# Attention stage on half slots: the two maps of a unit apart, negated maxima, roots on VectorE, the second half's units further apart

## The chip, the cores and the metric

One Trainium2 chip, one of its cores. The metric is the device time of one execution in microseconds; lower is better. TensorE (PE), VectorE (DVE), ScalarE (ACT), GpSimd (POOL) and the DMA queues run at the same time; each works through its own instruction list in order and waits for the others through semaphores. SyncE (SP) only issues transfers here.

## The reference, cut to what matters

One layer on 512 prompt positions and on 8 samples of 16 positions each (with 256 cached positions), D_MODEL 1024, float32:

```python
h = rms_norm(x, norm1_g) * (1 + sc1) + sh1
proj = h @ w_in                        # 11264 columns: retention q k v gate, diff q k v, two gates
ret_o = rms_norm(retention(...)) * silu(rg)
dq = rope(rms_norm(dq, diff_qnorm_g)); dk = rope(rms_norm(dk, diff_knorm_g))   # groups of 64
# differential attention: 8 heads, two maps per head (64 columns each), values 128 wide
s = einsum(q, k) * 64 ** -0.5          # per map; masked block-causally, chunks of 64
p = softmax(s); a = p[map 0] - lam * p[map 1]; diff_o = a @ v
diff_o = rms_norm(diff_o, diff_subln_g) * (1 - lam_init)
merged = sigmoid(g0) * (ret_o @ w_br_ret) + sigmoid(g1) * (diff_o @ w_br_diff)
x = x + gt1 * (merged @ w_out)
h2 = rms_norm(x, norm2_g) * (1 + sc2) + sh2
x = x + gt2 * hierarchical_moe(h2, ...)   # 16 experts, top-1 group, top-2 experts
```

The rotated keys, the values and the retention states are outputs as well.

## The kernel before, in words

The program has a retention phase (`phase_r`), then `phase_d`, which holds the attention stage, the output projection with the second norm and the router, and the experts. The change lies in the attention stage of `phase_d`, from about 777 us to 1190 us of the span.

**Groups, steps and slots.** In that stage TensorE works through nine projection groups (`DIFF_GROUPS`: K0, V0, Q1, K1, V1, GD0, GD1, BR0, BR1), each 512 columns wide: the diff-attention keys, values and queries of head halves 0 and 1 (four heads each; Q0 comes from the phase before), the gate of that branch in two halves, and the branch's output projection in two halves. A group has 8 row blocks k times 5 row tiles t (4 of the prompt, 1 of all samples) = 40 steps. A step (`step`, `mm3`) is three matmuls of 128x128 by 128x512 in split single precision (high x high, high x low, low x high) into bank `pj[t]`. Weights arrive in pieces of 128 x 1024 values, of which ScalarE makes the high part (`split_hi`) and GpSimd the low part by a subtraction (L1889).

Two steps are a slot; 20 slots are a group. Ahead of every slot TensorE calls `attend(s)`, and the other engines walk through the same slots, so the attention work is laid between the projection steps by a timetable written out by hand: class `Attention`, one object for each head half. For a slot it tells which unit is scored, turned, valued and so on. The class `Jobs` walks through the same slots once and numbers all the small TensorE jobs, each with one of the three small banks `B[0..2]` and its turn in it; `job_done` waits until TensorE has finished a job, `job_taken` until its bank was read. Since every engine's list is in slot order, an instruction that waits holds all that stands behind it on its engine.

**A unit** is one head and one query tile: 16 for each half, unit u has head u % 4, query tile u // 4 and (u // 4 + 1) x 128 keys.
- `scores` (L2430 on): for both maps a matmul with 64 rows of contraction (partitions 0 to 63 for map 0, 64 to 127 for map 1) and a mask matmul over the last 64 keys, into banks 0 and 1; the two maps' matmuls stand next to each other in the list.
- `maxima` (VectorE): two reduces and one scaling by -SCALE (L2172, L2174). `exps` (ScalarE): two exponentials with row sums (L1946), map 1 always into `E[:, 2]`, map 0 into `E[:, u % 2]`. `combine` (VectorE, L2180 to L2182): reciprocals, lambda factor, and the weighted sum of both maps.
- `turn` (TensorE, L2448): transposes; `take_A` (ScalarE, L1954) copies them; `values` (L2458) multiplies by the values; `take_o` (VectorE, L2190) scales into `o`; `square_o` (ScalarE, L1961) sums squares for the norm.

Half 0 scores a unit every 2 slots from slot 42 on, half 1 every slot from slot 102 on; the turn comes 3 and 2 slots after the scores, the values one slot later.

**The samples** follow unit 15 of each half, eight of them every two slots: `turn_keys` transposes 256 cached keys, `s_scores`, `s_maxima`, `s_exp`, `s_scale`, `s_turn`, `s_fold`, and for each pair of samples `s_values`. Cached keys and values come by transfers (`load_kc`, `load_vc`) into one buffer each.

**Rows and norms.** Q and K groups are taken out of the banks by ScalarE (`take_rows`, a square and a copy for each tile), summed by VectorE (`head_squares`), rooted (ScalarE's Sqrt, then `rsqrt_steps` on VectorE, L115 to L123) and rotated (`rotate`, one tile every two slots), then transposed at the slots in `turns`. The output norm does the same for each half in two parts (`o_variance`, `o_root`, `o_norm_root`, `o_norm`), and `out` has the slots at which its tiles are transposed for the branch projection. ScalarE loads a function table (ACT_TABLE_LOAD) whenever it goes from Exp, Sigmoid or Sqrt to another of these.

## Time and profile before

| | us |
|---|---|
| median of 3 runs | 1673.2 (1672.86 to 1677.64) |
| profiled execution | 1674.01 |
| its span | 1672.2 |
| TensorE busy | 1519.2 (91%) |
| VectorE busy | 825.7 (49%) |
| ScalarE busy | 665.5 (40%) |
| GpSimd busy | 355.2 (21%) |

The span runs from the first to the last instruction; the device time has 1.8 us more around it. The durations of matmuls are modelled and overlap in the pipeline (a 512-wide projection matmul shows 0.39 us), so cost is read from the start of one to the start of the next. The mean granted TensorE clock of the span is 0.960 of full speed. In the profile PE is the matmuls, PEld the weight loads; `d_B` are the small banks, `d_sm` the unit's maxima and sums, `d_E` the maps, `d_AT` the turned map, `ring_*` the weight pieces.

### The profile page before, as it was taken

What the parts mean: (1) busy time and instruction counts of PE and PEld (TensorE: products, weight loads), DVE (VectorE), ACT (ScalarE), POOL (GpSimd) and SP (SyncE); (2) the same over time, 40 slices, a digit from 0 to 9 for tenths busy, and PEclk for the clock granted to TensorE, in tenths of its full rate; (3) what the DMA queues carried; (4) which work ended last, traced back from release to release, by engine and by line L of the source; (5) the groups of instructions that cost most, each with busy time, mean ns of one, the idle gap of its engine ahead of it and who ended that gap; (6) DMA issues with size and microseconds to landing.
All of it is one profiled execution on the core that took longest, in us unless ns stands there. A gap on an engine that the chain in (4) does not pass through costs nothing.

```text
span 1672.2 us, 21251 instructions
## 1 busy us (share of the span) xinstructions
PE 1519.2 (91%) x7820; PEld 1140.6 (68%) x7820; DVE 825.7 (49%) x1370; ACT 665.5 (40%) x1085; POOL 355.2 (21%) x197
## 2 busy tenths in 40 slices
PE   4999999999999999997998788889999699999991
PEld 3675777577747764786875566767778578877871
DVE  3332341234123312222846664643445689998894
ACT  5312311221123112322344343564222268888881
POOL 1341123123312321333331111111430300000002
PEclk8999999999999999998999999999999599999995
DMA  9434452346136423424331144124661499999985
GB/s 342 127 89 139 149 181 73 126 152 197 53 126 194 157 78 131 158 76 151 94 114 38 39 139 145 58 77 152 251 172 51 132 337 360 392 394 390 386 326 201
DMA packets 158091, 290.31 MB, mean 174 GB/s; under 512 B 15084, under 2 KB 40860, under 8 KB 157734
## 3 DMA queue, kind: packets, MB, share of 16 engines
q1 hardware_dynamic: 154246, 278.47, 49.3%
q0 software_dynamic: 3744, 10.49, 1.7%
q8 instruction: 64, 1.05, 0.3%
q14 instruction: 37, 0.30, 0.1%
HBM read 251.55 MB, written 40.52 MB: 175 GB/s over the span
## 4 chain that ended last, share of the span: by engine, by line
PE 28%; DMA 9%; DVE 8%; ACT 4%; issue 3%; SPq 1%; DVEq 0%; ACTq 0%; POOL 0%; POOLq 0%
PE pj L93 7%; PE pj L95 7%; PE pj L94 7%; DMA m_raw<-w 6%; DVE d_tmp L2161 1%; DVE d_sm L2172 1%; ACT d_E L1946 1%; PE d_B L2439 1%; PE d_B L2466 1%; PE d_B L2500 1%; ACT m_hi L1362 1%; DMA d_kc<-cache_diff_k 1%; PE d_B L2458 1%; PE d_B L1537 1%; PE d_B L2477 1%
## 5 line engine op out<-in xcount | busy, mean ns | idle before, releaser
L93 PE MATMUL pj<-ring_hi,hT_hi 128*128 128x512 f32 x880 | 370.5, 421 | 20.6 <-ACT d_q_rows L1924 9.9
L95 PE MATMUL pj<-ring_hi,hT_lo 128*128 128x512 f32 x880 | 348.8, 396 | 0.0
L94 PE MATMUL pj<-ring_lo,hT_hi 128*128 128x512 f32 x880 | 348.2, 396 | 0.0
L464 POOL TENSOR_TENSOR ring_lo<-ring_raw,ring_hi 128x1024 fp32r<-128x1024 f32 x79 | 190.9, 2418 | 555.1 <-ACT ring_hi L530 555.1
L530 ACT ACTIVATE ring_hi<-ring_raw 128x1024 fp32r<-128x1024 f32 x79 | 83.5, 1059 | 427.8 <-DMA ring_raw<-w_in 361.9
L1441 DVE TENSOR_TENSOR m_lo<-m_raw,m_hi 128x1024 fp32r<-128x1024 f32 x188 | 224.2, 1222 | 23.9 <-ACT m_hi L1362 21.3
L93 PEld LDWEIGHTS pj<-ring_hi,hT_hi 128*128 128x128 f32 x880 | 168.5, 191 | 80.3 <-issue 34.7
L1362 ACT ACTIVATE m_hi<-m_raw 128x1024 fp32r<-128x1024 f32 x188 | 194.2, 1058 | 26.6 <-DMA m_raw<-w 24.1
L95 PEld LDWEIGHTS pj<-ring_hi,hT_lo 128*128 128x128 f32 x880 | 167.9, 191 | 37.9
L94 PEld LDWEIGHTS pj<-ring_lo,hT_hi 128*128 128x128 f32 x880 | 169.0, 192 | 30.4 <-issue 1.0
L1889 POOL TENSOR_TENSOR ring_lo<-ring_raw,ring_hi 128x1024 fp32r<-128x1024 f32 x37 | 89.9, 2433 | 362.8 <-ACT ring_hi L1909 362.8
L719 DVE SCALAR_TENSOR_TENSOR r_S<-r_S,g,r_sm 128x512 f32<-128x512 f32 x64 | 45.3, 745 | 124.1 <-PE r_sm L969 124.0
L93 PE MATMUL pj<-m_hi,m_xT_hi 128*128 128x512 f32 x248 | 98.8, 398 | 0.0
L95 PE MATMUL pj<-m_hi,m_xT_lo 128*128 128x512 f32 x248 | 97.2, 392 | 0.0
L94 PE MATMUL pj<-m_lo,m_xT_hi 128*128 128x512 f32 x248 | 97.1, 391 | 0.0
L93 PE MATMUL pj<-ring_hi,r_oT_hi 128*128 128x512 f32 x160 | 64.5, 403 | 5.0 <-issue 5.0
L1909 ACT ACTIVATE ring_hi<-ring_raw 128x1024 fp32r<-128x1024 f32 x37 | 39.1, 1057 | 73.1 <-DMA ring_raw<-w_in 25.5
L1335 POOL DMA_INDIRECT m_xe<-xg,m_si x16 | 16.5, 1033 | 240.7 <-PE d_B L1529 222.3
L94 PE MATMUL pj<-ring_lo,r_oT_hi 128*128 128x512 f32 x160 | 62.6, 391 | 0.0
L95 PE MATMUL pj<-ring_hi,r_oT_lo 128*128 128x512 f32 x160 | 62.4, 390 | 0.0
L1946 ACT ACTIVATE d_E<-d_B,d_sm 128x128 f32<-128x128 f32 (+3 forms) x64 | 33.2, 524 | 62.0 <-DVE d_sm L2174 62.0
L95 PEld LDWEIGHTS pj<-m_hi,m_xT_lo 128*128 128x128 f32 x248 | 46.9, 189 | 10.1
(341 smaller groups left out, 2428.4 us busy)
## 6 DMA issues: line engine op xcount, KB each, us to landing
m_raw<-w SPq DMA_DIRECT2D x188, 512.0 KB, 10.8
ring_raw<-w_in SPq DMA_DIRECT2D x72, 512.0 KB, 3.8
r_S<-state_ret SPq DMA_DIRECT2D x64, 256.0 KB, 4.7
r_ada_raw<-w_ada SPq DMA_DIRECT2D x16, 1024.0 KB, 6.7
o_state_s<-r_S SPq DMA_DIRECT2D x64, 256.0 KB, 4.8
a_raw<-w_ada SPq DMA_DIRECT2D x8, 1024.0 KB, 11.9
ring_raw<-w_in SPq DMA_DIRECT2D x32, 256.0 KB, 3.1
ring_raw<-w_br_ret SPq DMA_DIRECT2D x16, 512.0 KB, 4.0
```

Source lines behind the costliest of these rows:

```text
L93: pe.matmul(out, s_hi, m_hi, start=start, stop=False)
L94: pe.matmul(out, s_hi, m_lo, start=False, stop=False)
L95: return pe.matmul(out, s_lo, m_hi, start=False, stop=stop)
L464: pool.tensor_tensor(lo[:, p], raw[:, p], hi[:, p].bitcast(F32), ALU.subtract).then_inc(lo_done, 1)
L530: act.activation(hi[:, p], raw[:, p], ACT.Copy).then_inc(hi_done, 1)
L719: dve.scalar_tensor_tensor(S[:, u % 8], S[:, u % 8], K.g16[:, h:h + 1], job_bank("U", h, u)[:], ALU.mult, ALU.add) \
L1362: act.activation(self.hi[self.slot(n)][:], self.raw[self.slot(n)][:], ACT.Copy).then_inc(self.hi_done, 1)
L1441: dve.tensor_tensor(self.lo[s][:], self.raw[s][:], self.hi[s][:].bitcast(F32), ALU.subtract).then_inc(self.lo_done, 1)
L1537: last = pe.transpose(self.AT[:, a * P:(a + 1) * P], self.su[:, a * P:(a + 1) * P], K.ident[:])
L1889: pool.tensor_tensor(lo[:, p], raw[:, p], hi[:, p].bitcast(F32), ALU.subtract).then_inc(lo_done, 1)
L1909: act.activation(hi[:, p], raw[:, p], ACT.Copy).then_inc(hi_done, 1)
L1946: act.activation(E[:, u % 2 if m == 0 else 2, 0:nk], job_bank("S", i, u, m)[:, 0:nk], ACT.Exp, scale=SCALE, bias=sm[:, u % 4, 2 + m:3 + m] ...
```

## The change

The timetable counts in steps (half slots, 0 to 359) instead of slots. `place(h)` gives the old slot for even h and -2 for odd h, so work tied to a slot of a group stays where it was. In half slots, counted from the first scores of a unit:

| | before, half 0 | before, half 1 | after, both |
|---|---|---|---|
| map 1 / map 0 scored | 0 / 0 | 0 / 0 | 0 / 1 |
| combined | 2 | 2 | 3 |
| turned | 6 | 4 | 6 |
| valued | 8 | 6 | 8 |
| first unit, distance | 84, 4 | 204, 2 | 84, 4 and 194, 3 |

The samples' stream of half 1 starts at 246 (was 240); from the turn of a sample's keys, scores come at 3 (2), turn at 9 (6), values at 17 (14). The last output tile of half 1 is turned at 302 (298). `SCALE` goes into the query gains, so neither the exponentials nor the maxima scale; the maximum reduces write negated values themselves. Map 1's exponentials go to `E[:, 2]` and, for odd units, into half of the cached-value buffer `vc`, which is therefore loaded only after the last unit is combined. Every inverse root of the stage is made on VectorE from a bit pattern and three Newton steps, without ScalarE's Sqrt. Gate half 0 (GD0) is copied raw at the start of GD1, and both gate halves get their sigmoid at the start of BR0. GpSimd's `block_q` for half 1 moves from group GD1 to GD0.

```diff
+def rsqrt_bits(dve, links, out, var, tmp):
+    links(dve.tensor_scalar(tmp.bitcast(I32), var.bitcast(I32), 1, None, ALU.logical_shift_right))
+    links.sync()
+    links(dve.tensor_scalar(out.bitcast(I32), tmp.bitcast(I32), -1.0, float(0x5F3759DF), ALU.mult, ALU.add))
+    links.sync()
+    for _ in range(3):
+        links(dve.scalar_tensor_tensor(tmp, out, -0.5, out, ALU.mult, ALU.mult))
+        links.sync()
+        links(dve.tensor_tensor(tmp, tmp, var, ALU.mult))
+        links.sync()
+        links(dve.scalar_tensor_tensor(out, tmp, 1.5, out, ALU.add, ALU.mult))
+        links.sync()
...
-SLOTS = 20
+STEPS = KT * NT
+BETWEEN = -2
+def place(h):
+    return DIFF_GROUPS[h // STEPS], h % STEPS // 2 if h % 2 == 0 else BETWEEN
...
-        self.first, self.step, self.lag = ((42, 2, 3), (102, 1, 2))[i]
-        self.cache = (76, 120)[i]
+        self.first, self.period = ((84, 4), (194, 3))[i]
+        self.cache = (152, 246)[i]
...
+    def scored(self, h, m):
+        return self.unit(h, 1 - m)
+    def combined(self, h):
+        return self.unit(h, 3)
+    def turned(self, h):
+        return self.unit(h, 6)
+    def valued(self, h):
+        return self.unit(h, 8)
...
+        def exp_of(u, m):
+            return E[:, u % 2] if m == 0 else E[:, 2] if u % 2 == 0 else vc[:, 1, 0]
...
                     j = half.s_valued(s)
-                    if some(j) and (j + 1 < DEC_B // 2 or i == 0):
-                        load_vc(*((i, j + 1) if j + 1 < DEC_B // 2 else (1, 0)))
+                    if some(j) and j + 1 < DEC_B // 2:
+                        load_vc(i, j + 1)
+                    if half.combined(s) == U - 1:
+                        sp.wait_ge(A_done, (i + 1) * U)
+                        load_vc(i, 0)
...
-                    elif name in ("GD1", "BR0"):
-                        j = int(name == "BR0")
-                        take(f"GD{j}", lambda t: sg[:, t, j * W:(j + 1) * W], ACT.Sigmoid)
+                    elif name == "GD1":
+                        take("GD0", lambda t: sg[:, t, 0:W], ACT.Copy)
+                    elif name == "BR0":
+                        take("GD1", lambda t: sg[:, t, W:], ACT.Sigmoid)
+                        for t in range(NT):
+                            bank_taken(act, "GD0", t)
+                            act.activation(sg[:, t, 0:W], sg[:, t, 0:W], ACT.Sigmoid).then_inc(gate_done, 1)
...
                     if some(half.turned(s)):
                         take_A(i, half.turned(s))
-                    if some(half.scored(s)):
-                        exps(i, half.scored(s))
+                    for a in (1, 0):
+                        if some(half.scored(s, a)):
+                            exps(i, half.scored(s, a), a)
+                    if some(half.valued(s - 3)):
+                        n = half.valued(s - 3)
+                        square_o(i, n, o[i][:, n // HH, n % HH * P:(n % HH + 1) * P])
...
-            def maxima(i, u):
-                nk, c = unit_of(u)[2], sm[:, u % 4]
-                for m in range(2):
-                    job_done(dve, "S", i, u, m)
-                    links(dve.tensor_reduce(c[:, m:m + 1], job_bank("S", i, u, m)[:, 0:nk], AX, ALU.max))
-                links.sync()
-                dve.tensor_scalar(c[:, 2:4], c[:, 0:2], -SCALE, None, ALU.mult).then_inc(nmax_done, 1)
+            def maximum(i, u, m):
+                job_done(dve, "S", i, u, m)
+                dve.tensor_reduce(sm[:, u % 4, 2 + m:3 + m], job_bank("S", i, u, m)[:, 0:unit_of(u)[2]], AX, ALU.max, negate=True) \
+                   .then_inc(nmax_done, 1)
...
-            def scores(i, u):
+            def scores(i, u, m):
...
-                for m in range(2):
-                    pe.matmul(out[m][:, 0:nk], qT[i][part[m], h, t * P:(t + 1) * P], kT[i][part[m], h, 0:nk], start=True, stop=False)
-                for m in range(2):
-                    pe.matmul(out[m][:, nk - CHUNK:nk], mp[part[m], 0:P], mp[part[m], P:P + CHUNK], start=False, stop=True).then_inc(done, 1)
+                out, part = small("S", i, u, m), slice(m * DDH, (m + 1) * DDH)
+                pe.matmul(out[:, 0:nk], qT[i][part, h, t * P:(t + 1) * P], kT[i][part, h, 0:nk], start=True, stop=False)
+                pe.matmul(out[:, nk - CHUNK:nk], mp[part, 0:P], mp[part, P:P + CHUNK], start=False, stop=True).then_inc(done, 1)
...
             def attend(s):
                 for half in halves:
                     i = half.i
+                    for m in (1, 0):
+                        if some(half.scored(s, m)):
+                            scores(i, half.scored(s, m), m)
                     if some(half.valued(s)):
                         values(i, half.valued(s))
...
-                        if (k * NT + t) % 2 == 0:
-                            attend(g * SLOTS + (k * NT + t) // 2)
+                        attend(g * STEPS + k * NT + t)
```

## Rows read from the trace of the kernel before

**Rows 1.** Table by stretch, us: busy time and count per engine, clock, DMA share, GB/s.
```profile
849.64:890.13 40.49, 37.69 (x214) 29.16 (x212) 17.58 (x58) 17.13 (x60) 9.47 (x4) 1.00 0.26 83
890.13:952.89 62.76, 46.91 (x234) 33.54 (x233) 43.92 (x89) 26.78 (x73) 7.80 (x3) 0.92 0.09 26
952.89:1036.82 83.93, 72.22 (x614) 54.23 (x612) 49.23 (x121) 34.59 (x74) 12.18 (x5) 0.92 0.42 132
1036.82:1113.33 76.51, 65.45 (x411) 52.00 (x410) 40.29 (x115) 44.43 (x134) 10.88 (x6) 0.99 0.24 77
1113.33:1168.82 55.49, 53.98 (x528) 40.94 (x526) 24.05 (x76) 25.72 (x52) 9.53 (x4) 0.98 0.46 143
1168.82:1189.42 20.60, 18.88 (x94) 15.39 (x92) 5.42 (x15) 7.87 (x13) 4.81 (x2) 1.00 0.48 176
```
**Rows 2.** Timeline of TensorE at 793 us: start us, duration us, engine, line, operation.
```profile
793.16 0.39 PE L93 MATMUL pj<-ring_hi,hT_hi 128*128 128x512 f32 x1
...
793.85 0.39 PE L93 MATMUL pj<-ring_hi,hT_hi 128*128 128x512 f32 x1
```
**Rows 3.** Timeline of weight loads around the scores of two units (256, 512 keys).
```profile
871.68 0.30 PEld L2439 LDWEIGHTS d_B<-d_kT,d_qT 64*128 64x128 f32 x4
...
872.48 0.19 PEld L93 LDWEIGHTS pj<-ring_hi,hT_hi 128*128 128x128 f32 x1
...
932.94 0.97 PEld L2458 LDWEIGHTS d_B<-d_v,d_AT 128*128 128x128 f32 x8 [1.78 <-ACT d_AT L1954]
...
934.03 0.30 PEld L2439 LDWEIGHTS d_B<-d_kT,d_qT 64*128 64x128 f32 x4
...
935.26 0.19 PEld L93 LDWEIGHTS pj<-ring_hi,hT_hi 128*128 128x128 f32 x1
```
**Rows 4.** Timeline of weight loads of one sample slot.
```profile
1011.21 0.38 PEld L2500 LDWEIGHTS d_B<-d_vc,d_ATs 128*32 128x32 f32 x16 [0.36 <-issue]
...
1012.66 0.31 PEld L2487 LDWEIGHTS d_B<-ident,d_Ps 128*128 128x128 f32 x3 [0.20 <-issue]
1013.14 0.16 PEld L2477 LDWEIGHTS d_B<-d_kcT,d_qB 128*32 128x32 f32 x8 [0.17 <-issue]
...
1014.34 0.19 PEld L93 LDWEIGHTS pj<-ring_hi,hT_hi 128*128 128x128 f32 x1
```
**Rows 5.** Waits of 777 to 1210 us: waiter, releaser: total us, times, longest.
```profile
ACT d_E L1946 <- DVE d_sm L2174: 62.0, 29, 6.3
ACT d_Ps L1977 <- DVE d_sms L2198: 48.7, 16, 4.8
...
PE d_B L2458 <- ACT d_AT L1954: 14.7, 9, 4.9
```
**Rows 6.** Timeline of VectorE between the starts of two rotations, 512 keys.
```profile
933.28 1.29 DVE L2161 TENSOR_TENSOR d_tmp<-d_q_rows,d_tabs 128x512 f32<-128x512 f32 x2
...
936.27 1.28 DVE L2172 TENSOR_REDUCE d_sm<-d_B 128x1 f32<-128x512 f32 x2
...
939.33 0.17 DVE L2180 RECIPROCAL d_sm<-d_sm 128x2 f32<-128x2 f32 x1 [1.58 <-ACT d_E L1946]
...
940.46 1.29 DVE L2161 TENSOR_TENSOR d_tmp<-d_q_rows,d_tabs 128x512 f32<-128x512 f32 x2
```
**Rows 7.** Timeline, all engines, around one of GpSimd's subtracts.
```profile
872.27 2.40 POOL L1889 TENSOR_TENSOR ring_lo<-ring_raw,ring_hi 128x1024 fp32r<-128x1024 f32 x1 [7.13 <-ACT ring_hi L1909]
...
872.58 0.76 DVE L2172 TENSOR_REDUCE d_sm<-d_B 128x1 f32<-128x256 f32 x2 [0.44 <-PE d_B L2441]
...
873.37 1.32 DVE L2174 TENSOR_SCALAR d_sm<-d_sm 128x2 f32<-128x2 f32 x1
```
**Rows 8.** Groups of ScalarE, 777 to 1210 us: busy us, mean ns, idle before.
```profile
L1983 ACT ACT_TABLE_LOAD x4 | 5.1, 1283 | 0.1
```
**Rows 9.** Timeline of ScalarE, gate tiles of GD1.
```profile
1165.48 1.78 ACT L1931 ACTIVATE d_sg<-pj 128x512 f32<-128x512 f32 x3
```
**Rows 10.** Chain of waits, the transfer of a sample's cached keys.
```profile
989.39 4.92 DMA d_kc<-cache_diff_k
```

More of the change, by code:

```diff
@@ L1094, in __init__ @@
+        self.out = ((248, 252, 256, 264, 272), (280, 282, 284, 286, 302))[i]
         self.bank = (((0, 1, 2, 0, 1), (2, 0, 1, 2, 0)), ((1,) * NT, (0, 1, 2, 0, 1)))[i]
         self.out_bank = ((1,) * NT, (0, 2, 0, 2, 1))[i]
-    def unit(self, s, first):
-        u = s - first
-        return u // self.step if u >= 0 and u % self.step == 0 and u // self.step < UNITS else None
-    def scored(self, s):
-        return self.unit(s, self.first)
-    def turned(self, s):
-        return self.unit(s, self.first + self.lag)
@@ L1107, in valued @@
-    def valued(self, s):
-        return self.unit(s, self.first + self.lag + 1)
-    def stream(self, s, after, every=2, count=DEC_B):
-        b = s - self.cache - after
-        return b // every if b >= 0 and b % every == 0 and b // every < count else None
-    def keys_turned(self, s):
-        return self.stream(s, 0)
-    def s_scored(self, s):
-        return self.stream(s, 1)
-    def s_turned(self, s):
-        return self.stream(s, 3)
-    def s_valued(self, s):
-        return self.stream(s, 7, 4, DEC_B // 2)
@@ L1126, in rows_turned, with unit @@
-    def rows_turned(self, s, a):
-        return self.turns[a].index(s) if s in self.turns[a] else None
-    def out_turned(self, s):
-        return self.out.index(s) if s in self.out else None
+    def unit(self, h, after):
+        u = h - self.first - after
+        return u // self.period if u >= 0 and u % self.period == 0 and u // self.period < UNITS else None
+    def scored(self, h, m):
[4 more added lines that the diff above has]
+        return self.unit(h, 6)
@@ new lines, in valued, with stream, keys_turned, s_scored @@
+    def valued(self, h):
+        return self.unit(h, 8)
+    def stream(self, h, after, every=4, count=DEC_B):
+        b = h - self.cache - after
+        return b // every if b >= 0 and b % every == 0 and b // every < count else None
+    def keys_turned(self, h):
+        return self.stream(h, 0)
+    def s_scored(self, h):
+        return self.stream(h, 3)
+    def s_turned(self, h):
+        return self.stream(h, 9)
+    def s_valued(self, h):
+        return self.stream(h, 17, 8, DEC_B // 2)
@@ L1133, in some, with rows_turned, out_turned @@
+    def rows_turned(self, h, a):
+        return self.turns[a].index(h) if h in self.turns[a] else None
+    def out_turned(self, h):
+        return self.out.index(h) if h in self.out else None
 def some(n):
@@ L1804, in _ @@
             load_kc(0, 0)
-            load_vc(0, 0)
-            for s in range(SLOTS * len(DIFF_GROUPS)):
-                name, m = DIFF_GROUPS[s // SLOTS], s % SLOTS
+            for s in range(STEPS * len(DIFF_GROUPS)):
+                name, m = place(s)
                 if m % 5 == 4 and (name != "BR1" or m < 10):
@@ L1996, in _ @@
             take_rows(0, 0)
-            for s in range(SLOTS * len(DIFF_GROUPS)):
-                name, m = DIFF_GROUPS[s // SLOTS], s % SLOTS
+            for s in range(STEPS * len(DIFF_GROUPS)):
+                name, m = place(s)
                 if m == 0:
@@ L2045, in _ @@
                         take_O(i, half.out_turned(s))
[L2046 to L2049 removed]
+                    if some(half.s_scored(s - 2)):
+                        s_exp(i, half.s_scored(s - 2))
             def take_merged(t):
@@ L2249, in _ @@
             constants_ready()
-            for s in range(SLOTS * len(DIFF_GROUPS)):
-                name, m = DIFF_GROUPS[s // SLOTS], s % SLOTS
+            for s in range(STEPS * len(DIFF_GROUPS)):
+                name, m = place(s)
                 norm = {"K0": (0, 0), "V0": (0, 1), "K1": (1, 0), "V1": (1, 1)}.get(name)
@@ L2522, in attend @@
                         turn_out(i, half.out_turned(s))
-                    if some(half.scored(s)):
-                        scores(i, half.scored(s))
                     if some(half.turned(s)):
```

139 lines of the change are left out of this document (59 added, 80 removed).

## The prediction

> **What bounds the kernel now.** I read the page first: TensorE is busy 91% of the span, so it is the engine to follow, and its weakest slices lie in the middle, where the attention stage runs. Then the table by stage [rows 1]. I cut the stage at half slots (numbered 0 to 359 as in the new code, one per projection step of three matmuls), found by the first score matmul of a unit and the output turns: half slots 84 to 120 (A), 120 to 152 (B), 152 to 200 (C), 200 to 244 (D), 244 to 280 (E), 280 to 304 (F). For each I ask what TensorE would need if it never waited. A step costs 0.69 us from one first matmul to the next [rows 2]. A 128-wide pass of values or transposes costs 0.11 (eight loads in 0.97, of which one alone is 0.19, [rows 3]); so values and the turn of a unit with n key tiles cost 0.22n and 0.11n, a turn of rows 0.44, a turn of cached keys 0.81 (both counted in such passes). The sample stream's values, turn and scores cost 1.45, 0.48 and 1.20 [rows 4]. The scores of a unit, both maps, take 0.80 at 256 keys and 1.23 at 512 [rows 3], so 0.59, 0.80, 1.01, 1.23 for 1 to 4 tiles. By the timetable: A is 36 steps, scores of units 0 to 8, values 0 to 6, turns 0 to 7: 24.8 + 6.6 + 2.2 + 1.3 = 34.9. B is 32 steps, scores 9 to 15, values 7 to 14, turns 8 to 15: 22.1 + 8.0 + 5.7 + 3.1 = 38.9. C is 48 steps, values 15, eight samples and nine turns of rows: 33.1 + 0.9 + 25.7 + 4.0 = 63.7. D is 44 steps, 16 units, one turn of rows, keys twice and one sample's scores: 30.4 + 14.5 + 8.8 + 4.4 + 0.4 + 2.0 = 60.5 (a stage's last digit is rounded). E is 36 steps, the rest of the samples and five output turns: 50.7. F is 24 steps and five output turns: 18.8. Against 40.5, 62.8, 83.9, 76.5, 55.5 and 20.6 in [rows 1] the difference, waiting or half-speed work, is 5.6 + 23.9 + 20.2 + 16.0 + 4.8 + 1.8 = 72.3 us.
>
> What it waits for is in [rows 5]: values wait for ScalarE's copy of the turned map, and ScalarE has waited 62.0 us for VectorE's negated maxima and 48.7 for those of the samples. It is one ring through three in-order engines. In B it is plain [rows 6]: from one rotation's start to the next is 7.18 us, of which VectorE sits 1.58 waiting for exponentials that it made late itself; the two maxima, the scaling, both exponentials, the square and the copy stand one behind another, and only three slots are between the scores and the turn. The clock column of [rows 1] says that B and C ran at 0.92 of full speed, so some passes ran at 1.2 GHz after the longest waits: work at half speed is inside my 72.3.
>
> **The change, part by part.**
>
> *Maps apart: TensorE's cost.* This is the edit that speaks against the others. Before, the two maps' matmuls, each on 64 of 128 rows, are issued together. [Rows 3] show that they run at the same time: four passes of 512 columns and four of 64 need 4 x 0.43 + 4 x 0.05 = 1.92 us at the pitch of the 128-wide passes, and the whole takes 1.23 (256 keys: 1.07 against 0.80; four narrow weight loads are done in 0.30 us where eight wide ones take 0.97). Now the maps lie one step apart with full-height projection matmuls between them. What does one map alone cost? At least its own streaming: 2 x (n x 0.107) + 0.11, that is 0.32, 0.53, 0.75, 0.96, two of them being 0.05, 0.27, 0.48, 0.69 above the pair; over 8 units of each size +11.9 us. At most the same as the pair, if the pair's length is one map's own chain of load, pass, load, pass: +0.59, 0.80, 1.01, 1.23, times 8 = +29.0 us. The upper end is nearer: 512 minus 256 keys is 0.43 = two passes' streaming, which leaves 0.37 in every unit that is not streaming and belongs to each map's chain, not to having two. I take +29.0.
> The Trainium skill (TensorE: Matmul & The Clock Gate, Part 3: Packing small matmuls) says that a weight load overlaps running matmuls only when it goes to other rows of the array, and that narrow matmuls on different row groups run concurrently; the trace agrees (0.80 us for what would be 1.07 in file). By it a lone map hides nothing, which is the +29 end; without it, the +12 end.
>
> *Maps apart, new lags: what waiting goes.* Each map now has its own maximum (negated by the reduce itself), exponential and bank; combining comes at +3 half slots, the turn at +6, the values at +8. In the first half that is the same lag and pace as before (4 steps), but the first map's maximum and exponential run while the second's scores are made. Removed from VectorE's chain: the 128x2 scaling, 0.17 us, and 1.32 when GpSimd's subtract is running [rows 7]. After the second map's scores follow 0.44 until VectorE starts [rows 7], one reduce (0.64), one exponential with its sum (0.8, half of the 1.58 of [rows 6]) and the copy (0.6, as a 512-wide pass of [rows 9]) = 2.5 us, beside 3 steps, the next unit's first scores and a turn, 2.07 + 1.23 + 0.44. So in a plain stretch nothing is late.
> A: 5.6 goes to 1 (part of it was one table load, 1.28, ahead of the first exponential).
> B: VectorE's sum per unit at 512 keys with a rotation is reduces 1.28, rotation and taking of values 3.0, combining 1.4 = 5.7 us [rows 6]; TensorE's with doubled scores 4 x 0.69 + 2.45 + 0.88 + 0.44 = 6.5. TensorE sets the pace, and waits remain at the Q1/K1 edge (ScalarE takes five tiles in ten 512-wide passes, 5 to 6 us by [rows 9], with five 512-wide reduces beside them; I estimate 2 to 3 us of wait) and for GpSimd's 2.4 us subtracts [rows 7], three in the stretch: 23.9 goes to 6.
> C: sample exponentials move two half slots later, the turn to +6 after its scores instead of +4, values to +17. The ring gains 1.4 us of cover. VectorE with a rotation needs about as long per sample as in B, 6 us (estimate: rotation 2.7, and maximum, scaling, fold and norm at some 0.5 to 1 each), TensorE 4 x 0.69 + 0.81 + 1.20 + 0.48 + half of 1.45 + 0.44 = 6.4: close, so each blocked VectorE operation shows. With the edge at V1: 20.2 goes to 11.
> D: the second half's units lie 3 steps apart instead of 2 (16 units over half slots 194 to 247), lag 3 slots instead of 2. TensorE needs 2.07 + 2.45 + 0.88 + 0.44 = 5.8 at 512 keys, VectorE 3.0 (the 5.7 of B without its rotation), ScalarE 1.58 + square 0.5 + copy 0.6 = 2.7: nothing but TensorE is late. 16.0 goes to 3 (copies of V1 at 200, POOL).
> E: 4.8 to 3.5; the waits for cached keys' transfers stay.
>
> *Roots on VectorE.* 11 small operations of 0.17 to 0.2 us (the smallest row of VectorE in [rows 6]) replace 5 and a Sqrt on ScalarE. Table loads of 1.28 us go with it: there are 16 in the stage, in six groups of which [rows 8] is the first (lines 1926, 1946, 1977 three each, 1931 two, 2018 one), and two of them stand in ScalarE's queue at the Q1/K1 edge. Two remain and one comes later, for the norm of x1, behind output matmuls. This is in the stage figures above. Longer VectorE chain at the edges: +1.3 each, beside ScalarE's copies. [Rows 7] show an operation of 0.17 us on VectorE taking 1.32 until GpSimd's subtract ends; eleven instead of five can each meet it, at most once per subtract, so up to 2.4 us for each of the four head roots, which I put inside the residuals of B and C.
> *Startup:* gains are scaled once more ahead of the tables, while everything waits for VectorE: +0.2.
> *GD0 taken raw, both sigmoids at BR0.* ScalarE does a table load and ten passes of 0.5 to 0.6 in a row, 1.3 + 5.1 = 6.4 us [rows 8, 9], at half slot 280, and behind them stands the copy of output tile 0 in bank 0, then VectorE's low part. The last sample turn, at 283, needs bank 0. It comes about 7.8 us after 280, TensorE would be there after 3.0. F: 1.8 goes to 5 (before, five sigmoids and a Sqrt).
> *V buffer as fifth map buffer:* the first cached values of each half are loaded after the last combining, at 147 and 242, and used at 169 and 263: over 20 steps, 14 us, for two transfers like the 4.92 us of [rows 10]; SP's queue behind it holds a ring piece due at once, at worst one VectorE lag, 1 us, hidden by GpSimd's distance. POOL's block of q for half 1 moves forward by one group, into free time.
> The remaining steps (turns of rows) keep their half slots; the last output tile moves from 298 to 302, two steps ahead of its reader.
>
> **Sum**, against the profiled execution (1674.0, span 1672.2): scores +29.0; waiting 72.3 to 1 + 6 + 11 + 3 + 3.5 + 5 = 29.5, so -42.8; startup +0.2. Net -13.6: span 1658.6, time 1660.4. The median of the runs shown is 0.8 lower: 1660. The later stages follow TensorE's progress through semaphores and are taken to move as they are.
>
> **Rivals.**
> (1) *A lone map costs only its streaming.* +12 instead of +29: 1643. For it: the 0.37 could come from two maps' loads taking turns; against: the second map starts with the first (0.30 us for all four loads), so they hardly do.
> (2) *Slower: the waiting stays where it is structural.* The doubled scores are paid in all 32 units, while the waits of B and C sit at group edges (ScalarE taking tiles in front of exponentials in its own queue) and behind rotations on VectorE, both left in place. If only A and D empty (to 1 and 4) and B, C keep 20 and 18, E 5 and F 7, 55 remain: -17.3 + 29 + 0.2 = +11.9, 1685. It decides once more than 43 of the 72.3 us remain. For it: VectorE is busy 43.9 of B's 62.8; against: 1.58 us of every 7.18 is its own wait, and the slack of 0.8 us.
> (3) *The two cancel:* 40 to 47 remain, 1670 to 1677; the change moves waiting into matmuls.
> (4) *Nearly all waiting goes,* 15 remain: 1645.
>
> **Chances.** Forecast 0.52, (1) 0.12, (2) 0.19, (3) 0.10, (4) 0.07. A difference under 0.3%, 5 us, can't be told from none. Faster 0.70, same 0.11, slower 0.19. The forecast's own range, residual 22 to 38, is 1652 to 1668; with (1), (4) and (3) it is 1643 to 1677, and (2) is left out.
>
> **What would show it.** Score matmuls: one map's first load to the next projection load 0.8 us at 256 keys, 1.2 at 512, twice per unit (right); 0.53 and 0.96 is (1). Period in B near 6.5 with ScalarE no longer waiting 62 us. D without values waits, 75 us or so for the same steps. Table loads 3. Clock in B and C near 1.00. At BR0 a wait of some 5 us of the sample turn. Wrong if B and C keep their 147 us, or if a new wait on bank 2, which values and the next turn share one step apart, appears in D.

## The result and the profile after

| | before | after |
|---|---|---|
| median of 16 runs, us | 1676.1 (1672.3 to 1677.9) | 1679.8 (1677.1 to 1683.6) |
| profiled execution: span, us | 1672.2 | 1676.1 |
| ratio of the times, 95% interval | | 1.0027 (1.0019 to 1.0035) |

The forecast was 1660.0, in a range of 1643 to 1677; 1679.8 lies outside it. The medians differ by 3.7 us. That is inside the 0.3% that the prediction called "no change", but the interval leaves out 1, so the kernel became slightly slower where a gain of 13.6 us was forecast. (One execution, of the kernel "roots only" below, took 3841.6 us, more than twice the time of all others; its ratio leaves that execution out.)

First the page of the changed kernel: busy time by engine, TensorE by slice, and its clock.

```profile
PE 1546.2 (92%) x7820; PEld 1147.5 (68%) x7820; DVE 827.5 (49%) x1403; ACT 652.4 (39%) x1069; POOL 356.0 (21%) x197
PE   4999999999999999997999989998999699999991
PEclk9999999999999999999999989999999599999995
```

TensorE has the same 7820 matmuls and is busy 27 us longer, 1546.2 against 1519.2: waiting has turned into busy time. The table by stretch, in the six stages (columns as in [rows 1]):

```profile
851.98:897.10 45.12, 45.12 (x214) 32.87 (x212) 17.29 (x59) 17.32 (x61) 9.50 (x4) 1.00 0.22 74
897.10:951.62 54.52, 51.74 (x234) 35.60 (x233) 43.35 (x94) 23.77 (x66) 7.11 (x3) 0.97 0.12 38
951.62:1035.05 83.43, 74.50 (x634) 54.77 (x632) 52.27 (x139) 33.12 (x76) 13.40 (x7) 0.94 0.37 128
1035.05:1108.18 73.13, 73.11 (x345) 51.05 (x344) 34.93 (x102) 35.41 (x114) 9.49 (x4) 1.00 0.22 73
1108.18:1166.79 58.61, 55.24 (x523) 41.34 (x521) 26.22 (x75) 22.21 (x51) 9.53 (x4) 1.00 0.44 144
1166.79:1192.86 26.07, 21.54 (x147) 16.80 (x145) 8.07 (x27) 12.47 (x24) 4.79 (x2) 1.00 0.51 180
```

Beside [rows 1]: A takes 4.6 us more without one idle moment (45.12 of 45.12), B 8.2 less. C keeps its length although the second half's first units and one turn moved into it. D is 3.4 shorter, E and F are 3.1 and 5.5 longer (part of this is moved work: samples of half 1 start six half slots later). A to F sum to 340.9 us against 339.8.

Waits of the stage after, which answer to [rows 5] (waiter, releaser: total, times, longest):

```profile
ACT d_E L1968 <- DVE d_sm L2188: 49.7, 32, 3.7
ACT d_vc L1968 <- DVE d_sm L2188: 19.9, 8, 4.1
PEld d_B L2453 <- issue: 24.1, 64, 0.9
PE d_B L2500 <- ACT d_kcT L1990: 4.8, 1, 4.8
PE d_B L2471 <- ACT d_AT L1976: 0.5, 1, 0.5
```

The values' wait for ScalarE's copy of the turned map has gone from 14.7 us to 0.5. ScalarE itself still waits for the maxima, 49.7 us for the maps in `E` and 19.9 for those in `vc`, 69.6 together against 62.0 before. It was forecast to stop; what went is what TensorE had waited for behind it. The third row is the new one: 64 weight loads of scores, 0.38 us idle each, and no engine is named as releaser. What that is shows in TensorE's timeline of the changed kernel, around one map's scores at 512 keys (start us, duration):

```profile
943.77 0.39 PE L94 MATMUL pj<-ring_lo,hT_hi 128*128 128x512 f32 x1
943.99 0.40 PE L95 MATMUL pj<-ring_hi,hT_lo 128*128 128x512 f32 x1
944.32 1.12 PE L2453 MATMUL d_B<-d_kT,d_qT 64*128 64x512 f32 x2
945.28 0.33 PE L2454 MATMUL d_B<-d_mask_p 64*128 64x64 f32 x2
945.54 0.50 PE L93 MATMUL pj<-ring_hi,hT_hi 128*128 128x512 f32 x1
945.88 0.40 PE L94 MATMUL pj<-ring_lo,hT_hi 128*128 128x512 f32 x1
946.11 0.40 PE L95 MATMUL pj<-ring_hi,hT_lo 128*128 128x512 f32 x1
946.35 0.60 PE L2461 MATMUL d_B<-ident,d_E 128*128 128x128 f32 x4
946.70 0.47 PE L93 MATMUL pj<-ring_hi,hT_hi 128*128 128x512 f32 x1
947.01 0.39 PE L94 MATMUL pj<-ring_lo,hT_hi 128*128 128x512 f32 x1
```

From the first score matmul to the next projection matmul, 1.22 us: one map alone takes what both took together in [rows 3] (1.23). That was the forecast. But the pitch of projection matmuls (from the start of one to the start of the next) is 0.23, and here it is 0.33 on the way in (943.99 to 944.32) and 0.34 after the first one on the way out (945.54 to 945.88). From the last matmul ahead (943.99) to the second behind (945.88) is 1.88 us; less two plain pitches, 0.46, the lone map costs 1.42. That is 0.2 us beside its own length, and there are 64 such insertions instead of 32.

### The profile page after: what moved, and what is told of

Same layout as the page of the kernel before. It is cut to its first block, busy times and chain, and to the rows that moved or that the text cites. A ratio compares the mean times of both kernels' runs of the same rounds, so it can differ in the third digit from the quotient of the medians.

```text
span 1676.1 us, 21391 instructions
## 1 busy us (share of the span) xinstructions
PE 1546.2 (92%) x7820; PEld 1147.5 (68%) x7820; DVE 827.5 (49%) x1403; ACT 652.4 (39%) x1069; POOL 356.0 (21%) x197
## 4 chain that ended last, share of the span: by engine, by line
PE 33%; DMA 8%; DVE 7%; ACT 2%; issue 2%; SPq 1%; DVEq 0%; POOL 0%; ACTq 0%; POOLq 0%
PE pj L93 8%; PE pj L95 7%; PE pj L94 7%; DMA m_raw<-w 6%; PE d_B L2453 3%; PE d_B L2471 1%; DVE d_tmp L2179 1%; DMA d_kc<-cache_diff_k 1%; PE d_B L2479 1%; PE d_B L2461 1%; PE d_B L2454 1%; ACT m_hi L1385 1%; PE d_B L1560 1%; PE d_B L2513 1%; DVE m_oh L1467 0%
## 5 line engine op out<-in xcount | busy, mean ns | idle before, releaser
L93 PE MATMUL pj<-ring_hi,hT_hi 128*128 128x512 f32 x880 | 375.3, 427 | 20.1 <-ACT d_q_rows L1949 9.7
L95 PE MATMUL pj<-ring_hi,hT_lo 128*128 128x512 f32 x880 | 347.9, 395 | 0.0
L545 ACT ACTIVATE ring_hi<-ring_raw 128x1024 fp32r<-128x1024 f32 x79 | 83.4, 1059 | 422.3 <-DMA ring_raw<-w_in 359.3
L95 PEld LDWEIGHTS pj<-ring_hi,hT_lo 128*128 128x128 f32 x880 | 167.1, 190 | 37.5
L95 PE MATMUL pj<-m_hi,m_xT_lo 128*128 128x512 f32 x248 | 97.5, 393 | 0.0
L93 PE MATMUL pj<-ring_hi,r_oT_hi 128*128 128x512 f32 x160 | 64.5, 403 | 5.0 <-issue 5.0
L95 PE MATMUL pj<-ring_hi,r_oT_lo 128*128 128x512 f32 x160 | 62.3, 389 | 0.0
L2188 DVE TENSOR_REDUCE d_sm<-d_B 128x1 f32<-128x128 f32 (+3 forms) x64 | 31.2, 488 | 60.8 <-PE d_B L2454 60.8
L95 PEld LDWEIGHTS pj<-m_hi,m_xT_lo 128*128 128x128 f32 x248 | 47.0, 189 | 10.1
```

The costliest lines, as they stand in the source:

```text
L93: pe.matmul(out, s_hi, m_hi, start=start, stop=False)
L95: return pe.matmul(out, s_lo, m_hi, start=False, stop=stop)
L545: act.activation(hi[:, p], raw[:, p], ACT.Copy).then_inc(hi_done, 1)
L2188: dve.tensor_reduce(sm[:, u % 4, 2 + m:3 + m], job_bank("S", i, u, m)[:, 0:unit_of(u)[2]], AX, ALU.max, negate=True) \
```

## The experiments

"Stage" is half slots 84 to 304, from the profiled execution; it was 339.8 us before and 340.9 after. Ratios are to the kernel before, with a 95% interval. A stage is from one execution: over kernels of this table whose code for them is the same, B came out at 49.5 to 50.6 us, E at 58.0 to 61.2, and the rest of the span at 1333 to 1342. A difference of a few us between two stages alone tells little.

| kernel | median us | ratio | stage |
|---|---|---|---|
| maps together | 1653.9 | 0.9865 (0.9846 to 0.9884) | 319.9 |
| maps apart only | 1737.5 | 1.0367 (1.0348 to 1.0386) | 397.7 |
| roots only | 1673.1 | 0.9974 (0.9960 to 0.9988) | 334.9 |
| roots and negated maxima | 1661.9 | 0.9913 (0.9898 to 0.9928) | 324.2 |
| together, old gates | 1654.9 | 0.9870 (0.9851 to 0.9889) | 317.5 |
| together, half 1 quick | 1670.7 | 0.9959 (0.9946 to 0.9973) | 332.5 |
| together, whole maps | 1657.3 | 0.9884 (0.9865 to 0.9904) | 320.4 |
| together, sample turn earlier | 1674.6 | 0.9974 (0.9963 to 0.9986) | 336.9 |
| together, samples a step later | 1659.1 | 0.9893 (0.9878 to 0.9908) | 314.8 |
| together, norm root later | 1650.8 | 0.9851 (0.9831 to 0.9872) | 311.3 |
| after, norm root later | 1677.7 | 1.0006 (0.9994 to 1.0019) | 335.8 |

**Maps together.** All of the change, but TensorE issues both maps at one half slot.

```diff
-                    for m in (1, 0):
-                        if some(half.scored(s, m)):
-                            scores(i, half.scored(s, m), m)
+                    if some(half.paired(s)):
+                        scores(i, half.paired(s))
```

> The changed kernel, but TensorE issues map 0's scores beside map 1's again (same half slot); VectorE's and ScalarE's timetable stays as changed. Theory: the lone maps cost TensorE 28.6 us of lost overlap and about 0.2 us for each of the 32 extra breaks in the projection stream (6.4 us), so the time falls by 30 to 35 us against the changed kernel, to 0.980 to 0.984 of the kernel before; score pairs take 0.59, 0.80, 1.01, 1.23 us again. Rival: TensorE has slack here and the waits of the ring come back as soon as it is faster; the gain is under 12 us, ratio above 0.992.

Measured: 25.9 us faster than the changed kernel, and 1.35% faster than before. That is less than the 30 to 35 expected and far from the rival's 12. The rest of the change is a gain; the separation eats it. Its timeline at 512 keys:

```profile
928.19 0.40 PE L95 MATMUL pj<-ring_hi,hT_lo 128*128 128x512 f32 x1
928.52 1.13 PE L2458 MATMUL d_B<-d_kT,d_qT 64*128 64x512 f32 x4
929.48 0.34 PE L2460 MATMUL d_B<-d_mask_p 64*128 64x64 f32 x4
929.75 1.16 PE L2477 MATMUL d_B<-d_v,d_AT 128*128 128x128 f32 x8
```

Four matmuls in 1.23 us where the lone map needs 1.22 for two. The stage falls by 21.0 (in an execution that was 4.5 us above the median of its kernel), less than the 35.2 that the separation adds (28.8 + 6.4): some waits return, TensorE in B being busy 43.3 of 50.6 us.

**Maps apart only.** The kernel before, with map 1's scores one step later and nothing else.

```diff
                         if (k * NT + t) % 2 == 0:
                             attend(g * SLOTS + (k * NT + t) // 2)
+                        else:
+                            attend_other_map(g * SLOTS + (k * NT + t) // 2)
```

> The kernel before with one edit: TensorE issues map 1's scores one step after map 0's; all other engines' order and the timetable as before. Theory: +29 us of lost overlap and +6 of breaks, and the maxima start later, so 35 to 55 us slower, ratio 1.021 to 1.033. Rival (TensorE's extra work lies inside its waits, 72 us in this stage): under 15 us slower, ratio under 1.009.

Measured: +61 us, above the 35 to 55 expected. D alone has 41.6 of them (76.5 to 118.1). The table by stretch, first the whole of D and then a part of it:

```profile
1054.71:1172.81 118.10, 112.41 (x412) 79.74 (x411) 44.40 (x115) 43.98 (x133) 10.94 (x6) 0.71 0.16 50
1067.00:1134.80 67.80, 67.80 (x183) 47.90 (x184) 25.29 (x69) 17.73 (x68) 6.13 (x4) 0.51 0.11 35
```

This is not waiting: TensorE is idle for 5.7 us of D, less than the 11.1 of before. Its granted clock was 0.71, a mixture of 2.4 and 1.2 GHz, where it had been 0.99 [rows 1]. The clock fell after a wait of 2.3 us for exponentials that ended at 1064.0, and stayed at the lower level for 67.8 us in which no idle moment shows. There the pitch of projection matmuls is 0.43 (1102.78 to 1103.21) instead of 0.23. At the upper level the same work would have taken about half, so some 34 of the 41.6 us (an estimate from that row) are half speed. In the changed kernel the clock of D is 1.00. Whether the new lags, the wider spacing or the shorter chain on VectorE keeps it there was not tested one by one.

**Roots only** and **roots and negated maxima.** The kernel before with `rsqrt_bits` for all roots, then also with SCALE in the gains and reduces that negate.

```diff
-                dve.wait_ge(std_done, norm_index(i, a) + 1)
-                rsqrt_steps(dve, links, st[:, 3], st[:, 1], st[:, 2], st[:, 4])
+                rsqrt_bits(dve, links, st[:, 3], st[:, 1], st[:, 4])
...
-                links.sync()
-                dve.tensor_scalar(c[:, 2:4], c[:, 0:2], -SCALE, None, ALU.mult).then_inc(nmax_done, 1)
+                    dve.tensor_reduce(c[:, 2 + m:3 + m], job_bank("S", i, u, m)[:, 0:nk], AX, ALU.max, negate=True).then_inc(nmax_done, 1)
```

> The kernel before with the roots on VectorE from bits (no Sqrt on ScalarE in the stage), nothing else. Theory: 12 of 16 table loads go, of which about five stood in a wait of TensorE; 3 to 9 us faster, ratio 0.995 to 0.998, with the waits at the Q1/K1 and V1 edges 2 us shorter each. Rival: the eleven dependent VectorE operations take what the loads gave, ratio 0.999 to 1.002.

> As e3, and the maxima negated by the reduce, with the scale in the query gains. Theory: 32 + 16 operations of 0.17 us out of the ring, of which two were blocked by GpSimd to 1.3 and 1.6 us: a further 3 to 8 us, ratio 0.991 to 0.995. Rival: VectorE's ring has slack outside the rotations and only 1 to 2 us come, ratio 0.996 or more.

Measured: 0.26% for the roots, as expected, and 11 us more for the negated maxima, where 3 to 8 were expected; D is 71.5 and B 59.3 where the roots alone had 75.6 and 61.3. The 48 operations that are gone had taken 12.3 us on VectorE in the trace of before, not 48 times 0.17: most took 0.17, but four took 0.9 to 1.6, one of them the operation held by GpSimd's subtract in [rows 7]. The gain is about their whole length, so they stood in the chain that TensorE waited for.

**Insertions.** The kernel before with a small matmul in each of 18 steps without attention work.

```diff
+    for r in ((slice(0, P),), (slice(0, DDH),), (slice(0, DDH), slice(DDH, P)))[h % 3]:
+        pe.matmul(B[1 + (r.start > 0)][:, 0:CHUNK], mp[r, 0:P], mp[r, P:P + CHUNK], start=True, stop=True)
```

> The kernel before with one small insertion in each of 18 projection steps (half slots 42 to 59, no attention work there), three kinds in turn: one matmul on all 128 rows, one on 64 rows, and two side by side on the two halves, each 64 columns. It costs the time of a matmul result nobody reads. Theory 'half-height break' (the traces of before, after and e1 show a projection matmul next to a score insertion taking 0.33 instead of 0.23 us on either side): the full-height insertion costs little more than one small pass, about 0.05 to 0.1 us per step, the 64-row ones some 0.2 us more, and the pair costs nearly the same as the lone one. Rival 'any insertion breaks the stream': all three cost the same, 0.25 us or so. Rival 'the break is an artefact of long score passes': none costs more than 0.1 us. Read from the trace by the length of the step in which each lies; the total is at most 5 us more, too little to be read from the median.

TensorE's timeline, one cycle of the three kinds:

```profile
817.52 0.39 PE L95 MATMUL pj<-ring_hi,hT_lo 128*128 128x512 f32 x1
...
818.21 0.40 PE L95 MATMUL pj<-ring_hi,hT_lo 128*128 128x512 f32 x1
818.44 0.33 PE L2541 MATMUL d_B<-d_mask_p 128*128 128x64 f32 x2
818.58 0.47 PE L93 MATMUL pj<-ring_hi,hT_hi 128*128 128x512 f32 x1
818.89 0.40 PE L94 MATMUL pj<-ring_lo,hT_hi 128*128 128x512 f32 x1
819.13 0.40 PE L95 MATMUL pj<-ring_hi,hT_lo 128*128 128x512 f32 x1
819.46 0.43 PE L2541 MATMUL d_B<-d_mask_p 64*128 64x64 f32 x2
819.82 0.50 PE L93 MATMUL pj<-ring_hi,hT_hi 128*128 128x512 f32 x1
820.16 0.40 PE L94 MATMUL pj<-ring_lo,hT_hi 128*128 128x512 f32 x1
820.39 0.39 PE L95 MATMUL pj<-ring_hi,hT_lo 128*128 128x512 f32 x1
820.71 0.44 PE L2541 MATMUL d_B<-d_mask_p 64*128 64x64 f32 x4
...
821.65 0.39 PE L95 MATMUL pj<-ring_hi,hT_lo 128*128 128x512 f32 x1
```

Read it by the L95 rows: a step without insertion is 0.69 us, with 128 rows 0.92, with 64 rows 1.26, with 64 and 64 rows 1.26. So the insertions cost 0.23, 0.57 and 0.57 us. The theory holds in its order, not in its sizes (0.05 to 0.1 and some 0.2 more were expected): with the same columns a half-height insertion costs 0.34 more than a full-height one, and a second map beside it costs nothing. The rival "any insertion breaks the stream" is out. (The Trainium skill, TensorE: Matmul & The Clock Gate, Part 3: Packing small matmuls, says that narrow matmuls on different row groups run concurrently; this trace agrees, 0.57 for both.)

Where the 0.34 lies: 0.10 on the way in (0.33 from the L95 row to the insertion, against 0.23 for 128 rows), 0.22 in the two small passes (0.36 against 0.14), and only 0.02 to 0.03 on the way out (0.34 against 0.31). A wide gap behind an insertion is therefore no sign of a break by itself, since the full-height one has it too. The whole distance must be taken. In the changed kernel's timeline above, the four transposes (L2461), with a projection matmul ahead at 946.11 and the second behind at 947.01, cost 0.90 - 0.46 = 0.44 us: four passes of 0.11 [rows 3] and no break. The 35 lone maps that stand between two projection matmuls cost 0.79, 1.00, 1.21 and 1.42 us (medians for 1 to 4 tiles), a break of 0.2 in each. The kernel was timed once, 1681.6 us, which says nothing on so small a change; the reading is from the trace.

**Whole maps.** Both maps in one half slot, but scores, mask, scores, mask.

```diff
                     pe.matmul(out[m][:, 0:nk], ..., start=True, stop=False)
-                for m in (1, 0):
                     pe.matmul(out[m][:, nk - CHUNK:nk], ..., start=False, stop=True).then_inc(done, 1)
```

> The maps-together kernel with each map's two matmuls issued one behind the other (scores, mask, scores, mask) instead of interleaved (scores, scores, mask, mask), in one half slot. It tells whether the gain of a pair is adjacency or the order. Theory 'adjacency': the second map still streams beside the first, an insertion at 512 keys stays 1.23 us, 1654 +-2. Rival 'order': the mask pass of the first map, which waits for its own scores, stands in front of the second map's load, and the pair becomes two lone maps behind each other: 1.95 us at 512 keys, with one break instead of two, +20 us or more, 1675.

Measured: 1657.3, the insertion still 1.24 us at 512 keys in the trace, where the rival said 1.95. Adjacency counts, not the order inside; the median is 3.4 us above that of the interleaved order, but the intervals overlap.

**Half 1 quick.** Maps together, the second half's units as before: from half slot 204 on, two apart, with the old lags.

```diff
-        self.first, self.period = ((84, 4), (194, 3))[i]
+        self.first, self.period, self.lags = ((84, 4, (3, 6, 8)), (204, 2, (2, 4, 6)))[i]
```

> The maps-together kernel with the second half's units two half slots apart from 204 and lags of 2, 4 and 6 half slots, as before, instead of three apart from 194 with lags of 3, 6 and 8. Theory 'spreading is worth what stage D waits': before, D (200 to 244) held 16.0 us of waiting of which part was ScalarE and VectorE late by the short lags; with negated maxima, apart in the timetable, about half stays: +7 us, 1661, with values waits for the turned map's copy back. Rival 'spreading is worth nothing': the lags don't matter since negated maxima already shortened the chain, 1654 +-2. Rival 'spreading is the main gain': all 16 us and half-speed work return, 1670.

Measured: 1670.7, which is 16.8 us above the kernel with the maps together (7 were expected), and 12.6 us more in the stage. The rival "spreading is the main gain" had said 1670 and 16, and it fits. D by stretch:

```profile
1014.43:1097.67 83.24, 66.83 (x381) 49.42 (x380) 38.86 (x116) 37.77 (x127) 9.45 (x4) 0.98 0.24 75
```

16 us of its 83 are idle TensorE; in the quick timetable scores wait for exponentials (8.3 us) and turns for bank 2 behind VectorE (8.0 us, 0.54 in each of 15 units). The wait on bank 2 that the prediction named as a sign of being wrong shows here, not in D of the changed kernel. Spacing and lags were changed together, so the gain is that of both.

**Old gates.** Maps together, GD0 taken through the sigmoid at half slot 240 again.

```diff
-                        take("GD0", lambda t: sg[:, t, 0:W], ACT.Copy)
+                        take("GD0", lambda t: sg[:, t, 0:W], ACT.Sigmoid)
...
-                            act.activation(sg[:, t, 0:W], sg[:, t, 0:W], ACT.Sigmoid).then_inc(gate_done, 1)
```

> The maps-together kernel (1653.9 us, 0.9865 of before) with the gate sigmoids back where they were: the GD0 group taken through the sigmoid at half slot 240, nothing but GD1's five at 280. Theory: the ten passes behind one table load at 280 hold bank 0 and cost the last sample turn 3.6 us at half slot 283 and 2.3 at 280, so half slots 280 to 304 fall from 27.1 to about 23 and the whole to 1650 (0.984). The sigmoids at 240 cost one table load and no more than 1 us, since ScalarE has room there. Rival: the wait moves to 240, where samples start and ScalarE also copies keys: no gain, 1654. Rival 2: more than 27.1 minus 20.6 = 6.5 us comes back, 1647.

By the table by stretch, D and F:

```profile
1020.83:1085.34 64.51, 59.34 (x345) 44.86 (x344) 34.61 (x101) 37.91 (x117) 9.51 (x4) 0.97 0.26 82
...
1146.14:1169.64 23.50, 21.55 (x146) 16.81 (x145) 8.09 (x27) 9.88 (x19) 4.78 (x2) 1.00 0.57 199
```

F gives back 3.6 us (27.1 to 23.5), D takes 2.8 (61.7 to 64.5), and the time is the same, 1654.9 against 1653.9: the rival was right, and the 4 us that the theory expected did not come. The ten sigmoids at 280 are as expensive as expected and no worse than their old place.

**The wait at the V1 edge.** Three tries at the largest wait that is left, 4.8 us at half slot 161, where the first sample's turn waits for bank 0. First the turn two half slots earlier:

```diff
-        return self.stream(h, 9)
+        return self.stream(h, 7)
```

(the values two earlier as well).

> The maps-together kernel with the sample turn 7 half slots after the cached keys instead of 9, and the sample values 15 instead of 17. Its largest single wait, 4.8 us at half slot 161, is the first sample turn waiting for bank 0, which the keys turned at 160 hold and ScalarE copies only behind its ten passes over K1's tiles. At 159 the turn comes ahead of both. Theory 'bank link': 4.8 us go and the wait at the next keys stays under 2, C falls from 82.5 to 79, the whole by 3 to 4 us to 1650. Rival 'the chain is too short': scores to turn in 4 half slots instead of 6 leaves each of 16 turns waiting for VectorE's scaling by 0.5 us or more, +8 us, 1661. Rival 'the same work waits elsewhere': the copy of the turned map is what ScalarE then does behind its ten passes, 1654 +-2.

The wait moved to the next turn of rows (4.6 us), C grew from 82.5 to 90.7 and E from 61.2 to 68.5. Its waits, 932 to 1150 us:

```profile
DVE d_sms L2221 <- ACT d_Ps L2002: 16.7, 10, 2.9
...
PEld d_B L2506 <- DVE d_Ps L2223: 11.2, 7, 3.3
```

Turns wait for VectorE's scaling: the chain was made too short. The kind of the rival is right, the size is not (17 us in the stage and 20.7 in the median, where it said 8). Then the sample stream two half slots later:

```diff
-        self.cache = (152, 246)[i]
+        self.cache = (154, 246)[i]
```

> The maps-together kernel with the first half's sample stream two half slots later (154 instead of 152), everything else in place. Theory 'bank link': the turn of the first sample stands at 163 behind keys at 162, two steps (1.4 us) further behind ScalarE's ten passes at the V1 edge, so the 4.8 us wait falls to about 3.4, 1652.5. Rival 'the same work waits elsewhere': no change, 1654 +-2. If e9 gains and this doesn't, it is the order of the bank and not the distance that counts.

The 4.8 us wait is gone from the trace, but C stayed at 82.5, and the median is 1659.1, not the 1652.5 of the theory: the waiting came back elsewhere, as the rival said. Then I read in the changed kernel's trace what ScalarE waits for there: VectorE. VectorE's timeline of the changed kernel:

```profile
963.52 0.17 DVE L130 TENSOR_SCALAR d_so<-d_so 128x16 int32<-128x16 int32 x1
...
965.60 0.17 DVE L139 SCALAR_TENSOR_TENSOR d_so<-d_so 128x16 f32<-128x16 f32 x1
965.81 2.10 DVE L2162 TENSOR_REDUCE d_st<-d_tmp 128x8 f32<-128x512 f32 x3
```

Eleven operations in a row, 963.52 to 965.77, the root of the *output* norm, stand in front of the sums of K1's squares (L2162), and ScalarE's timeline has the answer:

```profile
966.59 0.60 ACT L1948 ACTIVATE d_tmp<-pj 128x512 f32<-128x512 f32 x1 [2.89 <-DVE d_st L2162]
...
969.47 1.14 ACT L1990 ACTIVATE d_kcT<-d_B 128x512 f32<-128x512 f32 x2
```

The last row frees bank 0. The weight loads of the changed kernel there:

```profile
970.24 0.50 PEld L2500 LDWEIGHTS d_B<-ident,d_Ps 128*128 128x128 f32 x3 [5.21 <-issue]
970.72 0.34 PEld L93 LDWEIGHTS pj<-ring_hi,hT_hi 128*128 128x128 f32 x1
```

After it loads take 0.34 instead of 0.19: TensorE came back at the lower clock (granted clock 0.51 from 970 to 976 us). Moving the root:

```diff
-                        if b == 0:
+                        if b == 1:
                             o_variance(i, 0)
-                        elif b == 1:
+                        elif b == 2:
                             o_norm_root(i, 0)
-                        elif b < 2 + NP_T:
-                            o_norm(i, b - 2)
+                        elif 3 <= b < 3 + NP_T:
+                            o_norm(i, b - 3)
```

> The maps-together kernel with the output norm's variance, root and four scalings each one sample later (four half slots). In its trace and in the changed kernel's, the root of the first half's output norm, eleven small operations on VectorE (2.3 us, 963.5 to 965.8 in the changed kernel), stands directly in front of the sums of K1's squares at the V1 edge; ScalarE waits 2.9 us for them with K1's tiles, copies the cached keys late, and TensorE waits 4.8 us for bank 0. Theory 'root in the way': with the root behind those sums the 4.8 us falls to about 2.5, C from 82.5 to 80, the whole from 1653.9 to 1651.5. Rival 'any VectorE work there is on the path': the root then delays the rotations behind it and comes back at a later sample, 1654 +-1. Rival 'bank link alone': ScalarE's ten passes (5 us) hold bank 0 anyway, and the wait at half slot 161 stays at 4.8.

> The changed kernel itself (maps apart) with the same move of the output norm's root by one sample. Theory 'root in the way': the wait at half slot 161 falls from 4.8 to about 2.5 us, C from 83.4 to 81, the whole from 1679.8 to 1677.5, so 1.001 of before. Rivals as in the kernel with the maps together: no change of the whole (1680), or no change of that wait.

Both came out as the first theory says: 1650.8 and 1677.7; the wait at 161 is 2.7 us in both, C 77.7 (from 82.5) and 80.5 (from 83.4). It is the wait and C that show it. In the medians the move gives 3.1 and 2.1 us, and the intervals with and without it overlap or touch. In the changed kernel with the move, TensorE's weight loads:

```profile
967.30 0.31 PEld L2500 LDWEIGHTS d_B<-ident,d_Ps 128*128 128x128 f32 x3 [3.12 <-issue]
```

and the table by stretch has C at clock 1.00 with the maps together, where it was 0.94 (in the changed kernel it is 0.96 with the move, so there a part stays at the lower clock):

```profile
937.02:1014.67 77.65, 69.40 (x634) 50.88 (x633) 51.34 (x139) 32.89 (x77) 13.46 (x7) 1.00 0.43 138
```

Maps together with the root moved has the lowest median of the study, 0.9851 of before.

## Why the prediction was wrong

In the prediction's own terms: it had 267.5 us of work without waiting, 29.0 for scores and 29.5 left of the 72.3, which is 326.0 for half slots 84 to 304. Measured, 340.9.

- **The failed step is the term "maps apart".** The lone map's own length was right: 0.585, 0.79, 1.01 and 1.22 us for 1 to 4 tiles, 8 x 3.6 = +28.8 against +29.0. Rival (1) is out. What the term left out is the break in the projection stream around a half-height insertion, 0.1 us beyond the pitch on either side of the length that I had read. 32 more insertions are +6.4 us, so the term was +35.2.
- **The same omission was in the 72.3.** The 32 insertions of before had their breaks too, 6.4 us, which I filed under "waiting or half-speed work" and let go with it. That left 65.9 for waiting and half speed. After, 340.9 - 267.5 - 28.8 - 12.8 (64 insertions' breaks) = 31.8 us remain, against 29.5 forecast. Waiting fell by 34.1, not by 42.8. Of the 14.9 missing, 12.8 are breaks, 2.3 are waits, and 0.2 goes the other way. The rows with the answer were on hand: in the timeline of before, around the scores at 256 keys of [rows 3], the last projection matmul ahead starts at 871.13 and the second behind at 872.82. Less 0.46 for two pitches and 0.22 for two passes of values, that is 1.01 us for the scores, where I had read 0.80. The samples' scores have such breaks as well (0.32 in and 0.34 out at 987.82 to 989.68 in the changed kernel), 16 of them or some 3 us, before and after alike; they are still inside the 65.9 and the 31.8.
- **A and B** were forecast at 42.5 and 52.9 (by the terms) and took 45.1 and 54.5, over by 2.6 and 1.6; the breaks of 18 and 14 insertions are 3.6 and 2.8. Their waits went as forecast, and a little further.
- **C to F** were forecast at 230.7 and took 241.2: those of 32 insertions make up 6.4, waits the other 4.1. I priced the longer root for the head norms only. The output norm's root, standing in front of K1's sums, held three engines; moved by one sample in the changed kernel, it gave 2.9 us in C. The gates cost what was said: ScalarE's table load and ten passes ran from 1167.8 to 1174.1, F has 5.4 us of excess for 5 forecast.
- **D** without values waits was right (73.1 of 73.1 busy), and spreading with the longer lags is worth 12.6 us in the stage and 16.8 in the median, by the quick timetable. The prediction's count for D before says "keys twice"; its sum has them once, as the trace does, so nothing hangs on it.
- **Table loads:** 2 in the stage instead of 16 (I said 3).
- **ScalarE** was to stop waiting 62 us for the maxima; it waits 69.6. The sign was badly chosen, since ScalarE can wait without holding TensorE.
- **Clock:** 0.97 and 0.94 in B and C, not "near 1.00". By the clock column half speed cost at most 0.03 x 54.5 + 0.06 x 83.4 = 6.6 us of the 31.8, and 13.6 of the 65.9 before by the same sum over [rows 1] (estimates: a stretch of length T at mean clock c loses (1 - c) T if TensorE is busy throughout).
- **Which rival.** By the prediction's own count 340.9 - 267.5 - 28.8 = 44.6 us of 72.3 remained, which is rival (3), the two cancel, and over the 43 at which (2) decides. I gave them 0.29 together. Against (2) I had argued from B, where I was right; the doubled scores were dearer than I knew. So (3) and (2) came near the time for another reason than theirs: of the 15.1 us that "remained" beyond 29.5, 12.8 were breaks, not structural waits.
- **Left open:** of the 3.7 us between the medians the stage shows 1.1. In the profiles the stage also begins 2.3 us later after the change, but over kernels with the same code up to there the start of K0 scatters from 785.3 to 788.4 us; whether the scaling of the gains costs anything wasn't separated.

## What to carry to other kernels

Count insertions into a dense matmul stream, not only their columns: price one by the distance between the last matmul ahead of it and the second behind it, against the plain pitch, because a part of its cost lies in its neighbours' rows. Keep two half-height matmuls adjacent: the second is free, and parting them has to save more waiting than its full length and a second break. When one engine takes over chains of small operations, look up what stands behind each chain in its queue at the group edges: with a chain of 2.3 us moved by one sample, TensorE's wait there fell from 4.8 to 2.7 us.

## What the runs showed of the hardware

- Two 64-row matmuls, in two halves of the array, cost the same as one: 0.57 and 0.57 us per small insertion, 1.23 and 1.22 at 512 columns, in either order of issue.
- A 64-row insertion among 128-row matmuls costs 0.2 us beyond its own length, 0.10 ahead of it and 0.11 behind; four 128-row transposes cost 0.44, their four passes, and no more. A small 64-row insertion costs 0.34 more than a 128-row one of the same columns.
- In "maps apart only" the granted clock fell after a wait of 2.3 us and stayed at 0.51 for 67.8 us in which TensorE shows no idle time, so a stretch of 118 us had 0.71 with TensorE busy 95% of it. Half-speed work counts as busy; the clock column must be read beside the busy one.
